# Three buffers for the dense u blocks, and every fifth split of a block on VectorE

## What is computed

```python
def peer_ffn(xn, w_q, keys1, keys2, u, v):
    ...
        s1 = jnp.einsum('thd,hnd->thn', q[..., :half], keys1).astype(jnp.float32)
        s2 = jnp.einsum('thd,hnd->thn', q[..., half:], keys2).astype(jnp.float32)
        v1, i1 = lax.top_k(s1, PEER_TOPK)
        v2, i2 = lax.top_k(s2, PEER_TOPK)
        ...
        g = jax.nn.softmax(sv, axis=-1)
        h = jax.nn.gelu(jnp.einsum('td,thkd->thk', xb, u[eidx]).astype(jnp.float32), approximate=False)
        return jnp.einsum('thk,thkd->td', (g * h).astype(v.dtype), v[eidx])
```

## Time and profile before

| | us |
|---|---|
| median of 3 runs | 3954.14 (3952.54 to 3961.48) |
| the profiled execution | 3955.22 |
| its span | 3953.4 |
| u stage in it | about 1704 to 2604 |

### The profile page before, as it was taken

One profiled execution on the slowest core, in us unless ns is written; L12 is line 12 of the kernel. 1 busy time (PEld: TensorE's weight loads), 2 busy tenths in 40 slices (PEclk: granted clock), 3 DMA queues, 4 the chain that ended last, 5 costly groups with the idle time before them and its releaser, 6 DMA issues. The chain is left out here.

```text
span 3953.4 us, 49767 instructions
## 1 busy us (share of the span) xinstructions
PE 3475.3 (88%) x17237; PEld 2505.3 (63%) x17237; DVE 2430.1 (61%) x5652; ACT 1160.2 (29%) x2266; POOL 1943.1 (49%) x1478
## 2 busy tenths in 40 slices
PE   7889886998989888888888877898689999999998
PEld 4445555788968767666666766665455656656655
DVE  3764423655857667788998887987533434434434
ACT  1213333121156523222222222266521222222222
POOL 0000001223400165778877788754267767777773
PEclk9888988998999999999999999999799999999999
DMA  3002103312431267899989999879898999999995
GB/s 117 10 33 61 55 27 124 101 54 85 139 100 33 72 229 252 338 348 370 398 335 364 362 391 402 336 259 405 315 359 334 375 354 341 372 356 348 360 368 218
DMA packets 335403, 978.48 MB, mean 248 GB/s; under 512 B 34400, under 2 KB 84456, under 8 KB 333648
## 3 DMA queue, kind: packets, MB, share of 16 engines
q0 software_dynamic: 156672, 570.49, 37.2%
q1 hardware_dynamic: 173584, 389.78, 27.9%
q10 hardware_dynamic: 4928, 15.34, 1.1%
HBM read 873.61 MB, written 101.89 MB: 247 GB/s over the span
## 5 line engine op out<-in xcount | busy, mean ns | idle before, releaser
L1609 PE MATMUL n_ps<-n_xh_flat,n_wh 128*128 128x512 f32 x3072 | 752.7, 404 | 132.0 <-POOL n_wh L1599 130.2
L2885 PE MATMUL e_y_ps<-e_wh,e_vh 128*128 128x512 f32 x3072 | 751.9, 401 | 46.1 <-DVE e_wh L3009 33.7
L1609 PEld LDWEIGHTS n_ps<-n_xh_flat,n_wh 128*128 128x128 f32 x3072 | 588.3, 194 | 290.6 <-POOL n_wh L1599 167.0
L2885 PEld LDWEIGHTS e_y_ps<-e_wh,e_vh 128*128 128x128 f32 x3072 | 572.8, 189 | 266.4 <-issue 118.5
L1025 POOL CAST m_wh<-raw 128x1024 fp32r<-128x1024 f32 x40 | 42.2, 1054 | 909.1 <-issue 657.2
L2969 POOL TENSOR_TENSOR e_vh<-raw,e_vh 128x1024 fp32r<-128x1024 f32 x128 | 309.5, 2421 | 224.2 <-ACT e_vh L2911 222.8
L3048 DVE TENSOR_TENSOR oT<-e_y_ps,oT 128x512 f32<-128x512 f32 x256 | 176.1, 691 | 376.6 <-PE e_y_ps L2885 375.2
L2544 POOL DMA_INDIRECT e_rows<-in_v,eid x346 | 348.2, 1006 | 99.2 <-issue 86.1
L1599 POOL TENSOR_TENSOR n_wh<-raw,n_wh 128x1024 fp32r<-128x1024 f32 x128 | 308.8, 2413 | 79.2 <-ACT n_wh L1594 77.3
L1946 DVE CUSTOM_DVE_ANT_0 oT<-oT,n_row_ps 128x1024 f32<-128x1024 f32 x222 | 265.5, 1216 | 60.4 <-DMA oT<-in_u,eid 57.3
L1062 PE MATMUL m_ps<-m_xh_flat,m_wh 128*128 128x272 f32 x1920 | 262.2, 299 | 40.6 <-DVE oT L1095 12.2
(11 more groups left out here) (390 smaller groups left out, 5713.5 us busy)
## 6 DMA issues: line engine op xcount, KB each, us to landing
raw<-in_ut SPq DMA_DIRECT2D x128, 512.0 KB, 5.5
raw<-in_v SPq DMA_DIRECT2D x126, 512.0 KB, 6.8
s_hid<-flat SPq DMA_DIRECT2D x128, 256.0 KB, 6.8
xrow<-s_hid SPq DMA_DIRECT2D x126, 256.0 KB, 8.4
s_gate<-g_stage SPq DMA_DIRECT2D x3, 8192.0 KB, 50.8
raw<-in_w_pq SPq DMA_DIRECT2D x32, 512.0 KB, 4.2
m_ring<-s_gate SPq DMA_DIRECT2D x32, 512.0 KB, 7.8
gh<-s_gate SPq DMA_DIRECT2D x32, 512.0 KB, 8.2
```

The costliest lines, as they stand in the source:

```text
L1609: mm = pe.matmul(self.ps[:, n % 2, 0:ND], self.uh[:, at % 2, a, k * P:(k + 1) * P], self.xd[:, b, k, :], start=(k == 0 and o == 0), stop=( ...
L2885: mm = pe.matmul(y_ps[:, o, 0:TD], vh[:, n % SLOT, a, m * P:(m + 1) * P], wh[n % SLOT][:, b, g * TD:(g + 1) * TD], start=(c == 0 and e == ...
```

## The change

There are now three buffers for a block and for its halves in place of two: the third block is in the tile `n_pt`, which the attention before has left, and its halves are in a new tile `u_third`. Round and split of block n+3 (not n+2) now follow product n. The load of block n+4 waits for the split of block n+1, not n+2. The gathers keep their rule (block n + 2.5), and so stand one split later in POOL's order. And the splits of the 24 blocks 5, 10, ... 120 are not POOL's any more: DVE makes them, in its own order, at the place where its estimated clock has reached block n - 1.5. They have a semaphore of their own, for which PE and SP wait at these blocks (`wait_split`). The clock of DVE's work in the stage grows by 24 x 1.3, from 784.0 to 815.2.

```diff
+DVE_SPLITS = tuple(range(5, 125, 5))
+U_CLOCK = 815.2
...
-    def __init__(self, mx, keep, dram, xd):
+    def __init__(self, mx, keep, dram, xd, third, third_loaded, dve_split):
         self.mx, self.keep, self.dram, self.xd = mx, keep, dram, xd
-        self.u, self.uh, self.hid, self.ps = keep["w"], keep["wh"], keep["out"], keep["mps"]
+        self.dve_split = dve_split
+        self.hid, self.ps = keep["out"], keep["mps"]
         self.blocks, self.products = mx.blocks_after, mx.products_after
+        self.u = [keep["w"][:, (self.blocks + b) % 2] for b in range(2)]
+        self.u.append(keep["pt"][:, :, :, :].rearrange("p a b c -> p (a b c)"))
+        self.uh = [keep["wh"][:, (self.blocks + b) % 2] for b in range(2)] + [third[:, :, :]]
         self.outs = 16 * (mx.passes_before + 1)
+        self.loaded = [mx.w_ready[(self.blocks + b) % 2] for b in range(2)] + [third_loaded]
+        self.loads_before = [(self.blocks + b) // 2 for b in range(2)] + [0]
+
+    def wait_split(self, engine, n):
+
+        if n in DVE_SPLITS:
+            engine.wait_ge(self.dve_split, DVE_SPLITS.index(n) + 1)
+        else:
+            engine.wait_ge(self.mx.w_split, self.blocks + n + 1 - sum(m < n for m in DVE_SPLITS))
 
     def load(self, sp, n):
-        at = self.blocks + n
-        sp.wait_ge(self.mx.w_split, at - 1)
-        sp.dma_start(self.u[:, at % 2], self.dram["ut"][n].rearrange("p k e -> p (k e)")
-                     ).then_inc(self.mx.w_ready[at % 2], 16)
+        if n < 2:
+            sp.wait_ge(self.mx.w_split, self.blocks + n - 1)
+        elif n == 2:
+            sp.wait_ge(self.mx.bank_free, self.mx.done(PKQ - 1))
+        else:
+            self.wait_split(sp, n - 3)
+        sp.dma_start(self.u[n % 3], self.dram["ut"][n].rearrange("p k e -> p (k e)")
+                     ).then_inc(self.loaded[n % 3], 16)
 
     def round(self, act, n):
-        at = self.blocks + n
-        act.wait_ge(self.mx.w_ready[at % 2], 16 * (at // 2 + 1))
-        act.wait_ge(self.mx.bank_ready, self.products + n - 1)
-        act.activation(self.uh[:, at % 2, HI, :], self.u[:, at % 2], ACT.Copy).then_inc(self.mx.w_high, 1)
-
-    def split(self, pool, n):
-        at = self.blocks + n
-        pool.wait_ge(self.mx.w_high, at - END + 1)
-        pool.tensor_tensor(self.uh[:, at % 2, LO, :], self.u[:, at % 2], self.uh[:, at % 2, HI, :].bitcast(F32),
-                           ALU.subtract).then_inc(self.mx.w_split, 1)
+        act.wait_ge(self.loaded[n % 3], 16 * (self.loads_before[n % 3] + n // 3 + 1))
+        if n != 2:
+            act.wait_ge(self.mx.bank_ready, self.products + n - (1 if n < 2 else 2))
+        act.activation(self.uh[n % 3][:, HI, :], self.u[n % 3], ACT.Copy).then_inc(self.mx.w_high, 1)
+
+    def split(self, engine, n):
+        engine.wait_ge(self.mx.w_high, self.blocks + n - END + 1)
+        engine.tensor_tensor(self.uh[n % 3][:, LO, :], self.u[n % 3], self.uh[n % 3][:, HI, :].bitcast(F32),
+                             ALU.subtract).then_inc(self.dve_split if n in DVE_SPLITS else self.mx.w_split, 1)
 
     def product(self, pe, n):
 
-        at, i = self.blocks + n, self.products + n
-        pe.wait_ge(self.mx.w_split, at + 1)
+        i = self.products + n
+        self.wait_split(pe, n)
         pe.wait_ge(self.mx.bank_free, i - 1 if n else i)
         for k in range(KD):
             for o, (a, b) in enumerate(PRODUCTS):
-                mm = pe.matmul(self.ps[:, n % 2, 0:ND], self.uh[:, at % 2, a, k * P:(k + 1) * P],
+                mm = pe.matmul(self.ps[:, n % 2, 0:ND], self.uh[n % 3][:, a, k * P:(k + 1) * P],
...
+            n_split = 0
             for cost in work():
                 clock[0] += cost * PIECE_SHARE
                 yield cost
+                while (u_began and n_split < len(DVE_SPLITS) and (clock[0] - u_began[0]) / U_CLOCK * (NKEY - 3)
+                       >= DVE_SPLITS[n_split] - 1.5):
+                    hidden.split(dve, DVE_SPLITS[n_split])
+                    n_split += 1
+                    clock[0] += 1.3
+                    yield 1.3
...
+        third = ctx.enter_context(nc.sbuf_tensor("u_third", [P, 2, D], F32R))
+        hidden = DenseHidden(mx, keep, dram, mx.xh, third, sem("r_u_third_loaded"),
+                             sem("r_u_dve_split"))
...
-            for n in range(2):
+            for n in range(3):
                 hidden.load(sp, n)
             for n in range(END - 3, END):
                 mx.store_pq(sp, n)
-            for n in range(2, 4):
-                hidden.load(sp, n)
+            hidden.load(sp, 3)
...
+            hidden.round(act, 2)
...
-                    if n + 2 < NKEY:
-                        hidden.round(act, n + 2)
+                    if n + 3 < NKEY:
+                        hidden.round(act, n + 3)
...
-            for n in range(2):
+            for n in range(3):
                 hidden.split(pool, n)
             for n in range(NKEY):
-                if n + 2 < NKEY:
-                    hidden.split(pool, n + 2)
+                if n + 3 < NKEY and n + 3 not in DVE_SPLITS:
+                    hidden.split(pool, n + 3)
```

More of the change, by code:

```diff
@@ L2224, in route @@
                 for i in range(n)]
-        hidden = DenseHidden(mx, keep, dram, mx.xh)
+        third = ctx.enter_context(nc.sbuf_tensor("u_third", [P, 2, D], F32R))
+        hidden = DenseHidden(mx, keep, dram, mx.xh, third, sem("r_u_third_loaded"),
+                             sem("r_u_dve_split"))
         spare = keep["mps"][:, 2, :]
@@ L2278, in _ @@
             assert n_step[0] == STEPS * QT
+            assert abs(clock[0] - u_began[0] - U_CLOCK) < 2, clock[0] - u_began[0]
         @block.sync
```

## The result

| | us |
|---|---|
| before, median of 4 runs | 3954.69 (3952.54 to 3961.48) |
| after, median of 4 runs | 4021.88 (4016.99 to 4029.12) |
| ratio | 1.0173, 95% interval 1.0160 to 1.0187 |
| span of the profiled execution after | 4014.8 |

The change makes the kernel 1.7% slower, 67 us, where 3940 was forecast and 3972 was the upper end of the range. All of it is there by the end of the u stage: the last gelu stands at 2671.8 us in place of 2604.2, and the last matmul of the last stage at 3983.7 in place of 3921.9.

What follows compares the result with a forecast made beforehand. POOL was taken to set the pace in the u stage's full stretches, DVE in the others. 3955.2 - 24 (POOL's relief) + 10 (DVE's splits) + 0 (third buffer) = 3941.2; as median 3940 us, range 3918 to 3972.

Steps and rivals of the forecast that it cites:

- What bounds the stage: u stage: POOL sets the pace in 500 us full of dots, DVE in the other 400; best read as DVE's ledger.
- The relief of POOL: 24 splits leave POOL, shortening the u stage's stretches full of dots: 24 us less, from 7.5 to 32.
- DVE's splits: 24 splits arrive on DVE at 1.55 us each; 10 us more in the sparse stretches, from 7 to 30.
- The third buffer: Splits made further ahead in the u stage: 0 us, since PE and POOL cannot use that lead; -11 as other end.
- What is queued behind the new waits: Product m waits for DVE, split m+3 and later gathers for product m; POOL's 15.7 us of work exceed the 11.
- Rival 1: PE is held by DVE's late splits at five places behind sparse stretches: +34 us on the forecast, 3974; chance 0.19.
- Rival 4: Each split of DVE meets one of POOL, 3.6 us each: slower, 3960 and up to 3965; chance 0.06.
- Rival 3: DMA is the ceiling at 398 GB/s: only 7.5 us come back, DVE takes 10; no change, 3957; chance 0.20.
- Rival 2: DMA's plateau is held and the third buffer's lead is used: -33 us, 3921; chance 0.13.

Runs made afterwards that it cites:

- e8_lead_only: The changed kernel with gathers up to block n + 3.5 behind each split, not n + 2.5: 3972.6 us, 1.0054 of the kernel before.
- e7_no_fifth_split: The changed kernel with the 24 splits of blocks 5, 10, ... 120 made by nobody: 3934.4 us, 0.9945 of the kernel before.
- e1_three_only: The changed kernel with all 128 splits on POOL again, three buffers kept: 3943.5 us, 0.9976 of the kernel before.
- e4_extra_dve: The kernel before with 24 subtractions of the same shape added on DVE, on tiles nobody waits for: 3974.4 us, 1.0055 of the kernel before.
- e5_split_earlier: The changed kernel with DVE's split of block m at block m - 4.5, not m - 1.5: 3937.8 us, 0.9958 of the kernel before.
- e2_two_buffers: The changed kernel with two buffers again, DVE's splits still at block n - 1.5: 4004.8 us, 1.0125 of the kernel before.
- e6_three_lead: The changed kernel with all splits on POOL, three buffers and gathers up to block n + 3.5: 3941.0 us, 0.9963 of the kernel before.

## Why the prediction was wrong

- **What bounds the stage** was read rightly as far as the runs show: DVE, with the gathers between POOL and DVE. With the splits at 0.5, 1.5, 3.0 and 4.5 the stage shortens with DVE's idle time before dots, and in `e8_lead_only` it does so while PE still stands for 132 us. The stages outside kept their lengths to within some 6 us.
- **The relief of POOL**, -24 with -7.5 to -32: measured 12 us (`e7_no_fifth_split` against `e1_three_only`), 3 to 22 by the intervals. About half the size, inside the ends. That DMA goes above 400 GB/s was right for some stretches; why POOL's 32 us in the full stretches gave no more was not settled.
- **DVE's splits**, +10 with +7 to +30: 22 us in `e4_extra_dve`, 5 us in `e5_split_earlier`. One took 1.30 us on average in the changed kernel, not 1.55; the 1.22 between the earlier trace rows was exact (median 1.222). What is added by meeting splits of POOL depends on the order: the average was 1.39 us in `e5_split_earlier`, 1.46 in `e8_lead_only` and 1.75 in `e4_extra_dve`.
- **The third buffer**, 0 with -11: -9.5 when nobody is held, so the -11 was near and the 0 was not. The reason given for 0 (PE and POOL cannot use the lead) does not hold: with PE held and the gathers where they stood, the third buffer gained 28 us (`e8_lead_only` against `e2_two_buffers`). That the changed kernel is 0.5% slower than `e2_two_buffers` comes from its later gathers.
- **What is queued behind the new waits: the step that failed.** The prediction named the chain rightly: product m waits for DVE, split m+3 and the gathers behind it wait for product m. It then weighed POOL's cover, 15.7 us of work, against the hold of PE, 11 us, and found it longer. But the cover must last until split m+3 can start, and that needs product m *done*, its bank read and the block rounded. At product 45 that is 13.7 (hold) + 8.2 (product, 2054.40 to 2062.56) + 1.6 (gelu and rounding) = 23.5 us from the end of product 44, against 14.6 us of work that POOL had: about 9 are missing, just the 9.03 us for which POOL is idle. With the prediction's own 11 and 5.5 us, and the 1.6 from the trace, it would have been 18.1 against 15.7: a loss already.
- **At how many places.** Rival 1 looked at one place in DVE's order behind a sparse stretch, found it 11 us late, and took that for the five such changes. The trace of before could have shown more: if the dots on either side of each place are timed against the end of product m-1, nine of the 24 places are late by 2.4 to 11.4 us (5, 15, 25, 30, 35, 45, 65, 85 and 120), and none of the others is clearly early. In the changed kernel PE was held at every one of the 24, 7.6 us on average.
- "The gathers keep their rule, and so stand one split later" was told as part of the change and **costed at nothing**. `e8_lead_only` undoes just that, and takes back 47 of the 67 us. Without a hold the same term is worth nothing that can be measured (`e6_three_lead` against `e1_three_only`): it costs only where PE is held.
- **The rivals.** Rival 1 had the mechanism, and with 0.19 too small a chance; its 3974 was 48 us short, since it counted five places. Rival 4 (each split meets one of POOL) falls: five of the 24 overlap one (the fifth by only 0.01 us), where three in ten was reckoned, and of these one took over 2 us (2868 ns). The Trainium skill's rule ("SBUF — State Buffer", "Who interferes with whom": the second instruction waits for the first) is borne out wherever two met. The 2868 ns end 1.1 us after POOL's split ends; three splits of POOL that began behind one of DVE's took 2614, 2663 and 3165 ns in place of 2408; and the longest (4241 ns) began 2.0 us before the end of another DVE instruction with two inputs. As a price per split of DVE it came to 0.08 us in the changed kernel, and to 0.5 in `e4_extra_dve`. Rival 3 (DMA the ceiling) falls as a ceiling at 398, with 410 GB/s over 100 us; its price for the relief, 7.5 us, lies within the 3 to 22 measured. Rival 2 (3921) was reached by nothing: 3934 is the time even where the 24 splits are made by nobody. Without the hold, `e5_split_earlier` took 3938 us, next to the forecast's 3940. That is in part luck: the relief was about half of what was forecast, and the third buffer, taken as 0, made up for it.

## What to carry to other kernels

Work that is moved into the written order of another engine must stand there before the moment at which its consumer wants it, and after its own input is there; time each such place against consumer and producer before anything else is summed. A cover is to be weighed against the whole way to the next instruction that can start (the wait, the producer's work behind it, the steps between), not against the wait alone. And when a step is moved ahead in a queue, the rule that places the others behind it has to be looked at again: here a lead of one block more gave back seven tenths of the loss, and with the splits placed early it did harm.

## What the runs showed of the hardware

**A hold costs PE twice.** The stretches around product 45, in the columns as above:

```profile
2041.00:2048.00 7.00, 0.00 (x0) 0.00 (x0) 6.90 (x53) 1.41 (x2) 5.63 (x6) 0.84 0.87 300
2048.00:2054.40 6.40, 0.00 (x1) 0.01 (x1) 6.40 (x26) 0.00 (x0) 5.61 (x5) 0.50 0.88 303
2054.40:2059.00 4.60, 4.60 (x11) 3.63 (x12) 4.60 (x20) 0.00 (x0) 0.76 (x1) 0.50 0.90 329
2059.00:2063.00 4.00, 4.00 (x19) 3.24 (x18) 4.00 (x10) 0.44 (x1) 0.00 (x0) 0.95 0.21 85
```

PE is idle from 2040.7 to 2054.4. In that time the granted clock falls to 0.50, the 1.2 GHz level, and stays there for the first 4.6 us of the product: 11 matmuls in 4.6 us, then 19 in 4.0 us. The product took 8.2 us in place of 5.5. Of the 24 products behind a hold 22 took 7.1 to 8.6 us, and two, behind holds of 1.0 and 3.2 us, took under 5.8; together they took 184 us where the same 24 took 141 before. Over the stage the granted clock was 0.89 where it was 0.97. On POOL's way to split 48 the 2.7 us of product 45 count in full.

**The stage begins later with a third buffer.** The last matmuls of the stage before and the first of the u stage, in the kernel after:

```profile
1699.64 8.55 PE L1062 MATMUL n_ps<-n_xh_flat,n_wh 128*128 128x512 f32 x37
1713.01 12.16 PE L1627 MATMUL n_ps<-n_xh_flat,n_wh 128*128 128x512 f32 x42 [4.82 <-ACT flat L1129]
```

The first gelu stands at 1722.5 us, at 1717.8 in `e1_three_only`, at 1711.3 before and at 1712.7 with two buffers. The load of block 2 now goes ahead of the last stores of the stage before, and ACT waits 2.9 us for one of these stores, which it did not before; that this load delays it was argued, not tested. In all kernels with three buffers the first gelu stands 6 to 13 us later than before, and nothing in the prediction foresaw that.
